# A two-layer decoder trunk: 96 slots an expert, a one-hot built earlier, and a combine in two rounded passes

## What is computed

```python
def moe(h, router_w, router_bias, w_gate, w_up, w_down):
    t = h.reshape(Bsz * T, D)
    scores = jax.nn.softmax(t @ router_w)
    # the best of 4 groups, and in it the two best experts of each token; their scores divided by their sum
    gate = jnp.sum(jax.nn.one_hot(idx, N_EXPERTS) * wk[..., None], axis=1)
    a = silu(einsum('td,edf->tef', t, w_gate)) * einsum('td,edf->tef', t, w_up)     # 1024 -> 512
    a = a * gate[..., None]
    return einsum('tef,efd->td', a, w_down)                                         # 512 -> 1024

def run_trunk(x, c, pos, attend, p):          # the frame of it
    for l in range(2):
        sh1, sc1, g1, sh2, sc2, g2 = ada_mod(c, ada_w[l], ada_b[l])
        h = x * (1 + sc1) + sh1
        out = chunk_gmlp(h, ...) if l == 0 else diff_out(attend(rope(h @ b_w_q), k_sh, v_sh, lam), ...)
        x = layer_norm(ALPHA * x + (1 + g1) * out)
        h = x * (1 + sc2) + sh2
        x = layer_norm(ALPHA * x + (1 + g2) * moe(h, ...))
        if l == 0: k_sh, v_sh = rope(x @ kv_w_k), x @ kv_w_v
```

## Time and profile before

| what | value |
|---|---|
| median of 3 runs | 1463.88 us (1462.59 to 1464.76) |
| the profiled execution | 1465.82 us, its span 1464.1 us |
| busy share of the span | PE 87%, DVE 59%, ACT 36%, POOL 2% |
| weight loads on PE (PEld) | 962.6 us, beside the matmuls |
| chain that ended last | PE 71%, DVE 19%, issue 4%, ACT 3% |
| the largest lines in it | L627 24%, L391 17%, L646 16% |
| DMA | 355.32 MB, mean 243 GB/s |

### The profile page before, as it was taken

How to read it: one execution, slowest core, us unless ns; L and a number is a source line. 1 busy time by engine, 2 the same in 40 slices (tenths; PEclk the granted TensorE clock), 3 DMA queues, 4 the chain that set the end, 5 groups by cost and what they waited for, 6 DMA issues and landing times.

```text
span 1464.1 us, 19293 instructions
## 1 busy us (share of the span) xinstructions
PE 1271.6 (87%) x7150; PEld 962.6 (66%) x7150; DVE 865.1 (59%) x1113; ACT 532.7 (36%) x613; POOL 24.9 (2%) x30
## 2 busy tenths in 40 slices
PE   4797877999999997899757989798688999999985
PEld 2695746888888885599323322226377888888864
DVE  1436474666666622744798899945666666666334
ACT  1333225555555512443111111113245555555321
POOL 2000001000000000000000000000010000000000
PEclk9899968999999997999857778888979999999988
DMA  9929532999999875544529888776309999999200
GB/s 332 386 107 344 172 116 75 353 332 337 339 335 338 297 280 181 180 142 146 193 96 322 297 307 299 284 271 228 117 0 344 340 335 337 334 334 338 105 2 30
DMA packets 143713, 355.32 MB, mean 243 GB/s; under 512 B 4706, under 2 KB 4899, under 8 KB 143652
## 3 DMA queue, kind: packets, MB, share of 16 engines
q1 hardware_dynamic: 142388, 350.91, 67.2%
q0 software_dynamic: 1264, 3.59, 0.8%
HBM read 351.20 MB, written 3.28 MB: 242 GB/s over the span
## 4 chain that ended last, share of the span: by engine, by line
PE 71%; DVE 19%; issue 4%; ACT 3%; SPq 2%; DMA 2%; ACTq 0%; POOL 0%; DVEq 0%
PE gu L627 24%; PE pj L391 17%; PE pj L646 16%; DVE wring L1816 4%; PE tb L425 4%; DVE tokB L1819 3%; PE tb L422 2%; PE gu L457 2%; PE pj L793 2%; DMA wring<-in_a_w_in 1%; SPq L890 1%; ACT whi L1215 1%; PE pj L491 1%; PE tb L565 1%; PE pj L402 1%
## 5 line engine op out<-in xcount | busy, mean ns | idle before, releaser
L1673 DVE TENSOR_TENSOR wlo<-wring,whi 128x2048 fp32r<-128x2048 f32 x128 | 289.9, 2288 | 111.6 <-ACT whi L1215 111.6
L1215 ACT ACTIVATE whi<-wring 128x2048 fp32r<-128x2048 f32 x128 | 244.3, 1914 | 150.0 <-PE gu L627 150.0
L646 PEld LDWEIGHTS pj<-tokB,wring 128*128 128x128 f32 x2048 | 233.5, 192 | 4.8 <-issue 2.1
L646 PE MATMUL pj<-tokB,wring 128*128 128x128 f32 x2048 | 233.9, 275 | 1.7 <-issue 1.7
L627 PE MATMUL gu<-whi,xhi 128*128 128x512 f32 x512 | 207.0, 404 | 13.7 <-DVE xlo L1699 13.7
L627 PE MATMUL gu<-wlo,xhi 128*128 128x512 f32 x512 | 203.9, 398 | 0.0
L627 PE MATMUL gu<-whi,xlo 128*128 128x512 f32 x512 | 203.7, 398 | 0.0
L1109 ACT ACTIVATE reg<-pj 128x264 f32<-128x264 f32 (+2 forms) x171 | 85.6, 512 | 312.7 <-PE pj L646 144.6
L793 PE MATMUL pj<-wring,ws 128*8 128x512 f32 x256 | 127.5, 658 | 1.0 <-DVE lamx L1895 1.0
L627 PEld LDWEIGHTS gu<-whi,xhi 128*128 128x128 f32 x512 | 97.9, 191 | 36.3 <-DVE xlo L1699 8.3
L627 PEld LDWEIGHTS gu<-whi,xlo 128*128 128x128 f32 x512 | 97.7, 191 | 22.5
(11 more groups left out here) (294 smaller groups left out, 1741.3 us busy)
## 6 DMA issues: line engine op xcount, KB each, us to landing
wring<-in_moe_w_gate SPq DMA_DIRECT2D x32, 2048.0 KB, 9.5
wring<-in_moe_w_up SPq DMA_DIRECT2D x32, 2048.0 KB, 10.3
wring<-in_moe_w_down SPq DMA_DIRECT2D x32, 2048.0 KB, 9.1
wring<-in_ada_w SPq DMA_DIRECT2D x24, 2048.0 KB, 13.3
wring<-in_cache_k SPq DMA_DIRECT2D x64, 512.0 KB, 5.0
wring<-in_cache_v SPq DMA_DIRECT2D x64, 512.0 KB, 5.0
wring<-in_a_w_in SPq DMA_DIRECT2D x4, 2048.0 KB, 20.1
wring<-in_a_w_out SPq DMA_DIRECT2D x2, 2048.0 KB, 16.8
```

What stands on the lines that cost most here:

```text
L646: m = pe.matmul(bank[:, i * P:(i + 1) * P], w[:, k, f * P:(f + 1) * P], aT[:, k, :], start=(k == 0), stop=(k == FB - 1))
L1215: act.activation(whi[q], quarter(wring, q, s), ACT.Copy).then_inc(hi_ready, 1)
L1673: dve.tensor_tensor(quarter(wlo, q, s), quarter(wring, q, s), whi[q].bitcast(F32), ALU.subtract).then_inc(lo_ready, 1)
```

## The change

- An expert's window is 96 columns (`WIN`) instead of 128. The pieces that follow from it (`xhi`, `xlo`, the rows of `gu`, `atok`, `aT`, the down result) shrink to 96. The passes for larger experts begin at 96.
- The gates and places are turned and spread in the last expert's step, and DVE's `put(k)` runs there too. It now builds a one-hot without weights (`putR`) and the gate of each slot (`gslot`).
- In the combine ACT scales a row tile by its gate while it rounds it (`yhi`), DVE makes the low part (`ylo`), and each group is 10 fp32r matmuls with `putR`. `ylo` lies in ring slots 3 and 4, so the loads behind it change slots, and two wait for the end of the combine. `ada_tile(1,1)` stands behind the combine, `mod_rows(1,1)` behind the residual.
- In the router ACT rounds quarters 0, 2 and 3 of expert 0's weights before the second token tile is evacuated and quarter 1 after it; DVE makes the low parts in the order 0, 2, 3, 1.
- At the start the load of ada(0,4) stands behind the four `a_w_in` tiles, POOL's loads wait for ada(0,3), and the transposes of `ws` and `ada_tile(0,4)` stand behind the first projection.

```diff
-SPAN = P
-PACK = SLOT_N + SPAN
+WIN = 96
...
-        yr = reg1[:, 0:NK * D].rearrange("p (k n) -> p k n", n=D)
-        put = hT[:, :, :].rearrange("p c t -> p (c t)")[:, 0:NK * T].rearrange("p (k t) -> p k t", t=T)
...
+        yhi = rounded("yhi", "reg1", 0, NK * D).rearrange("p (k n) -> p k n", n=D)
+        ylo = rounded("ylo", "wring", 3 * TILE, NK * D).rearrange("p (k n) -> p k n", n=D)
+        putR = rounded("put_rounded", "hT", 0, NK * T).rearrange("p (k t) -> p k t", t=T)
...
-        xhi = rounded("xhi", "tok4", 0, D).rearrange("p (c n) -> p c n", n=P)
-        xlo = rounded("xlo", "tok4", D, D).rearrange("p (c n) -> p c n", n=P)
+        xhi = rounded("xhi", "tok4", 0, C * WIN).rearrange("p (c n) -> p c n", n=WIN)
+        xlo = rounded("xlo", "tok4", D, C * WIN).rearrange("p (c n) -> p c n", n=WIN)
...
+            for n, s in enumerate((4, 5, 0, 1)):
+                project(s, "a_in", n == 0)
...
             for q in range(2):
                 small([((P, c * P, P), tr(ws[:, 4 * q + c, :])) for c in range(4)])
-            ada_tile(0, 4, 4)
-            for n, s in enumerate((5, 0, 1, 2)):
-                project(s, "a_in", n == 0)
-            at["uv"] = g.n
+            pe.wait_ge(pj_evac, g.n)
+            def beside():
+                ada_tile(0, 4, 2)
+                ada_tile(0, 5, 3)
+            norm(zT, beside, lambda: None)
             ada_turn(0, 4)
-            pe.wait_ge(pj_evac, g.n)
-            norm(zT, lambda: ada_tile(0, 5, 3), lambda: None)
             ada_turn(0, 5)
             ada_tile(0, 6, 4)
...
-                            m = pe.matmul(gu[q // 2][:, :], x[:, c, :], w[:, k, :],
+                            m = pe.matmul(gu[q // 2][0:WIN, :], x[:, c, :], w[:, k, :],
...
-                                m = pe.matmul(bank[:, i * P:(i + 1) * P], w[:, k, f * P:(f + 1) * P], aT[:, k, :],
+                                m = pe.matmul(bank[:, i * WIN:(i + 1) * WIN], w[:, k, f * P:(f + 1) * P], aT[:, k, :],
...
+                    if last:
+                        small([((6, P * j, n), tr(sg[0:n, j, :], n)) for j, n in enumerate(tiles)])
                     for q in range(4):
-                        part(q, s + q // 2)
+                        part(q, s + q // 2, not behind)
+                        if last and q in (1, 2):
+                            if q == 1:
+                                emptied()
+                            for i in (2 * q - 2, 2 * q - 1):
+                                small([((P, 0, T), mm(ident[0:4, i:i + 1].to_broadcast([4, P]), lgT[0:4, :]))])
...
-                    small([((P, f * P, P), tr(atok[:, f * P:(f + 1) * P])) for f in range(FB)])
+                    small([((P, f * WIN, WIN), tr(atok[0:WIN, f * P:(f + 1) * P], WIN)) for f in range(FB)])
...
-                step(3)
+                step(3, last=True)
...
-                small([((6, P * j, n), tr(sg[0:n, j, :], n)) for j, n in enumerate(tiles)])
-                emptied()
-                for i in range(4):
-                    small([((P, 0, T), mm(ident[0:4, i:i + 1].to_broadcast([4, P]), lgT[0:4, :]))])
                 for k in range(NK):
-                    n = P if k < NK - 1 else LAST
                     for q in range(2):
-                        turned(n, yg[:, 4 * q:4 * q + 4, k * P:k * P + n])
-                pe.wait_ge(pj_evac, g.n)
-                if l == 0:
-                    ada_tile(1, 1, 0)
+                        if 2 * k + q >= NBANK:
+                            pe.wait_ge(row_low, 2 * NK * l + 2 * k + q + 1 - NBANK)
+                        turned(P, yg[:, 4 * q:4 * q + 4, k * P:(k + 1) * P])
                 operand()
                 for c in range(C):
-                    group(P, T, [(yr[0:(P if k < NK - 1 else LAST), k, c * P:(c + 1) * P], put[0:(P if k < NK - 1 else LAST), k, :])
-                                 for k in range(NK)])
+                    def rows(j):
+                        if c == 0 and j % 2 == 0:
+                            pe.wait_ge(row_low, 2 * NK * l + max(2 * NK + 1 - NBANK, j + 1))
+                        elif c < NBANK and j == 0:
+                            pe.wait_ge(row_low, 2 * NK * (l + 1))
+                    group(P, T, [(y[:, k, c * P:(c + 1) * P], putR[:, k, :]) for k in range(NK) for y in (yhi, ylo)], rows)
                 at[f"moe{l}_end"] = g.n
...
-            ada_turn(1, 1)
+            ada_tile(1, 1, 0)
             ada_tile(1, 2, 1)
             def beside():
+                ada_turn(1, 1)
                 ada_turn(1, 2)
-                ada_tile(1, 3, 3)
+                ada_tile(1, 3, 5)
             norm(yT, beside)
             ada_turn(1, 3)
-            ada_tile(1, 4, 4)
-            for n, s in enumerate((5, 2, 0, 1)):
+            ada_tile(1, 4, 2)
+            for n, s in enumerate((3, 4, 0, 1)):
                 project(s, "kv", n == 0)
...
-            for n in range(2, 5):
+            for n in range(2, 4):
                 ada(0, n, n)
-            for n, s in enumerate((5, 0, 1, 2)):
+            for n, s in enumerate((4, 5, 0, 1)):
                 load(s, columns("a_w_in", n, 0))
-            for n, s in ((5, 3), (6, 4), (7, 5), (8, 2)):
+            for n, s in ((4, 2), (5, 3), (6, 4), (7, 5), (8, 2)):
                 ada(0, n, s)
...
-            for n, s in ((1, 0), (2, 1), (3, 3), (4, 4)):
+            for n, s in ((1, 0), (2, 1), (3, 5), (4, 2)):
                 ada(1, n, s)
-            for name, slots in (("kv_w_k", (5, 2)), ("kv_w_v", (0, 1))):
+            free[3] = free[4] = (pj_done, at["moe0_end"])
+            for name, slots in (("kv_w_k", (3, 4)), ("kv_w_v", (0, 1))):
                 for n, s in enumerate(slots):
                     load(s, columns(name, n))
-            for n, s in enumerate((3, 4)):
+            for n, s in enumerate((5, 2)):
                 load(s, columns("b_w_q", n, 0))
...
+            pool.wait_ge(slot_in[3], 16)
...
+                tokens(NB, 2)
+                tokens(P, 0)
+                for q in (0, 2, 3):
+                    high(q, 0, first=True)
+                tokens(P, 1)
...
+                act.wait_ge(pj_done, at[f"hT_read{l}"])
+                high(1, 0, first=True)
...
+                act.wait_ge(put_ready, l + 1)
                 for k in range(NK):
-                    n = P if k < NK - 1 else LAST
                     for q in range(2):
-                        evac_wide(yr[0:n, k, q * 512:(q + 1) * 512], n)
-                if l == 0:
-                    rows(1, 1)
+                        evac_wide(yhi[:, k, q * 512:(q + 1) * 512], P, ACT.Identity, scale=gslot[:, k:k + 1])
                 for c in range(C):
...
             moe(0)
             for _ in range(2):
                 tile_split()
+            rows(1, 1)
             rows(1, 2)
...
-                for q in range(4):
+                for q in (0, 2, 3, 1):
...
+                def put(k):
+                    mine = kst[:, K_PART + k:K_PART + k + 1]
+                    one_, two_ = first_of[k % 2], second_of[k % 2]
+                    dve.scalar_tensor_tensor(one_, sgB[:, 0, :], mine, sgB[:, 2, :], ALU.is_equal, ALU.mult)
+                    link(dve.scalar_tensor_tensor(two_, sgB[:, 1, :], mine, sgB[:, 3, :], ALU.is_equal, ALU.mult))
+                    link(dve.tensor_tensor(one_, one_, two_, ALU.add))
+                    dve.tensor_reduce(gslot[:, k:k + 1], one_, AX.X, ALU.add).then_inc(dve_own, 1)
+                    own.add()
+                    return dve.tensor_scalar(putR[:, k, :], one_, 0.0, None, ALU.not_equal)
...
+                    else:
+                        empty(dve.tensor_copy(lgT[0:6, :], batch()[0:6, 0:T]))
+                        for i in range(4):
+                            empty(dve.tensor_copy(sgB[:, i, :], batch()[:, 0:T]))
+                        last_empty()
+                        put(0)
+                        put(1)
...
+                    else:
+                        put(2)
+                        put(3)
...
+                ready(put(4))
+                dve.wait_ge(dve_own, own.value())
+                dve.nop().then_inc(put_ready, 1)
...
+                main = at[f"moe{l}_main"]
                 for k in range(NK):
-                    mine = kst[:, K_PART + k:K_PART + k + 1]
-                    dve.scalar_tensor_tensor(put[:, k, :], sgB[:, 0, :], mine, sgB[:, 2, :], ALU.is_equal, ALU.mult)
-                    link(dve.scalar_tensor_tensor(rs[:], sgB[:, 1, :], mine, sgB[:, 3, :], ALU.is_equal, ALU.mult))
-                    i = dve.tensor_tensor(put[:, k, :], put[:, k, :], rs[:], ALU.add)
-                    if k < NK - 1:
-                        link(i)
-                ready(i)
-                if l == 0:
-                    mod_rows(1, 1)
+                    for q in range(2):
+                        dve.wait_ge(pj_evac, main + 2 * k + q + 1)
+                        cols = slice(q * 512, (q + 1) * 512)
```

(2 more changed lines are left out.)

89 lines of the change are left out of this document (49 added, 40 removed).

## The result

The changed kernel took 1430.91 us (median of 4 runs, 1428.81 to 1432.07); the kernel before, on the same chip, 1464.32. The ratio is 0.977 (0.9754 to 0.9788): 33 us less. In the two profiled executions the span fell from 1464.1 to 1429.2, by 34.9; the one of before lay 1.5 us above its median.

The account below looks back on a forecast made before the run. PE was taken to bound the expert loop, with removed waits outside it worth their length. The terms A to F summed to -37.5 us, from 1463.88 to a median of 1426.4 us, range 1400 to 1442.

Parts of the forecast that it names:

- A: Expert loops at 96 columns: gate/up and down matmuls gain nothing, only activation transposes get shorter; -2.4 us (0 to -4.4).
- B: Start: the first a_in tile lands earlier, less an ada tile moved between the norm's statistics; -5.5 us (-9.5 to -3.5).
- C: Routers: PE's pick in layer 0 no longer stops, and smaller splits shorten each layer's ramp; -4.6 us (-9 to -1).
- D: Last expert's step in both layers: PE takes in three transposes and four fp32 matmuls; +4.4 us (+2 to +6).
- E: Last down pass to combine's end: gap plus 18.4 us with fp32r matmuls; -21.2 and -15.2 us (together -45 to -21).
- F: Behind layer 0's combine: ACT waits for the late kv load, second statistic at half clock; +7.0 us (0 to +14).
- R1: Rival: gate/up matmuls get faster with 96 stationary columns, 27 us more gained, 1399 us; chance 0.11.
- R2: Rival: the down pass shrinks with its streamed columns to three quarters, 57 us, 1369 us; chance 0.04.
- R4: Rival: in gate/up, a weight load of 96 columns is no longer hidden behind the stream, 95 us, 1521 us; chance 0.03.
- R5: Rival: an expert has over 96 tokens and takes the slow loop behind the branch, 750 us a layer; chance 0.01.
- R3: Rival: behind the loop, half clock through one combine (+7.8) and the kv wait at its upper end (+7), 1441 us; chance 0.15.

Follow-up runs that it names:

- e1: The changed kernel with the expert window back at 128 columns, all else as changed; 1436.96 us, ratio 0.9818.
- e2: The changed kernel with gate/up holding 32 stationary columns and down streaming 32, instead of 96, further tokens left out; 1566.08 us, ratio 1.070.
- e11: The changed kernel with gate/up holding 64 stationary columns and down streaming 64, instead of 96, further tokens left out; 1430.41 us in one run.
- e7: The changed kernel with ACT's four high parts of the first expert behind the second token tile again, DVE's low parts in order; 1436.89 us, ratio 0.9802.
- e8: The changed kernel with the first kv tile loaded into slot 5 during the last experts, ada(1,3) taking slot 3 behind the combine; 1424.09 us, ratio 0.9715.
- e12: The changed kernel with new slots for first kv and q tiles, DVE's low parts before mod_rows(1,0), two ada loads held until written keys land; 1414.06 us.
- e3: The changed kernel without the branch behind each loop and its passes for experts of more than 96 tokens; 1416.74 us, ratio 0.9683.

## Why the prediction was right

Point by point, in us:

| step | predicted | measured |
|---|---|---|
| A, loops | -2.4 | -2.5, from expert 1 to 14 alone |
| B, start | -5.5 | -5.9 to a_out |
| C, routers | -4.6 | -4.2 and -2.5 |
| D, last steps | +4.4 | +5.2 |
| E, combines | -21.2, -15.2 | -20.0, -15.6 |
| F, behind the combine | +7.0 | +9.2 |
| attention, not counted | 0 | +2.1 |
| tail, not counted | 0 | -0.8 |

The errors go both ways and cancel in part. C and the tail gave 2.9 more than counted; F, attention, D and E 5.9 less. So the sum is 2.6 off in the profiled executions and 4.5 in the medians.

A held in its rates, and e1, e2 and e11 show that the row with 9 columns was the right one to go by.

B held as a sum and not in its mechanism. The first a_in tile landed at 38.0 instead of 48.2, 10.2 us earlier where 7.4 were counted. It then no longer ended last: the fourth ada tile did, with its product on PE (3.51 us) and the modulation behind it, so the projection came 8.6 earlier. From there to a_out it took 2.7 more where 1.9 were counted.

C: layer 0 is the stop that e7 brings back. Layer 1 gave 2.0 more than counted; 1.8 of it lies between the first two experts. There seven of the kernels with 96 columns take 15.4 us and three take 16.9 with the same code. In the seven the granted clock is 1.00 through the first gate/up (11.4 us), in the three it is 0.50 for 3.4 us of it (12.9), and before the change it was 0.50 for 3.0 us. Which one a run gets no experiment here explains; the 1.8 are luck.

E: behind the gap the sum was 18.4 and the trace has 18.4 and 18.0; the gaps were 7.8 and 5.1. The step that was off is the gap in layer 0, taken as 6.6. It stayed near the 8.14 of before, with DMA moving 263 GB/s there. Inside the 18.4 the row tiles took 7.6 instead of 8.5, since the clock rose before their end, and the wait for DVE's last low rows took that back.

F is the mechanism that was written down, a wait for the kv load on ACT, and up to the squares it was sized right: they begin 12.8 us behind the combine's end (12.6 counted). The 3.8 for a second statistic at half clock went elsewhere: that statistic took 4.72 us instead of 3.83. PE's order was overlooked. PE stands for 5.15 us until ACT has evacuated the two rows that come behind the splits, then turns them and makes an ada tile at half clock (3.58 and 3.60 us; 1.85 and 1.90 in e8). So the statistic begins 6.7 us behind the squares, where it began 1.7 behind them before. Two of the prediction's own signs lie just outside for B and F: the first projection at 44.6 (46 to 48 said) and the root at 24.3 (18 to 24).

Attention has no term in the sum. With everything 20 us earlier and other slots, ada loads met the rows that are written and waited for, +4.0 (e12); 1.9 came back between there and layer 1's logits, which no run explains.

Of the rivals, R1 and R2 are out by e2 and e11. R4 and R5 didn't come: less weight was loaded faster (164 ns on average in a gate/up weight load, 191 before), and the passes were not taken (PE runs 7150 matmul instructions before and after). R3 didn't come: the combines' matmuls ran at full clock, and F was 2.2 above its term, not 7.

The rule that sustained work releases the slow clock (the Trainium skill, TensorE: Matmul & The Clock Gate, "Part 1: The HAM clock gate") was weighed for the combine and left out. The trace agrees with it: the clock was 0.50 for 5.6 us of the row tiles and 1.00 behind them. The 3 us that it was to bring didn't come, since DVE's low rows then end last; even e3, at full clock throughout, needs 17.1 us behind its gap. In e2 a PE that is busy all the time is slowed all the same.

## What to carry to other kernels

Before narrowing a matmul, find in the trace one of the same kind that is much narrower on that side: if its pace is the same, narrowing gives nothing but what is copied and turned around it. Work that a later stage needs and whose inputs are long known (here the one-hot) is worth moving under another engine's steady work, even at a price there: 3 us bought 14.3. When a buffer is borrowed from a ring of loads, list which loads wait for it and what stands behind them on every queue: the few lines of e8 to e12, most of all the kv tile's slot, gave back 15 us.
